# A hybrid layer pair in fp32 split form: triangular solve and state-space products in smaller array tiles, MLP loop written out

## The reference, cut to what matters

```
m = where(strict, einsum(kb, k) * decay, 0);  a_mat = m + eye(64)
sol = triangular_solve(a_mat, rhs, lower=True, unit_diagonal=True)
```

```
bu = einsum('bsgh,gph->bsgp', uf, b_bar)
states = associative_scan(combine, (lam_bar, bu))
y = einsum('bsgp,ghp->bsgh', states, c_mat).real + d * uf
```

## Time and profile before

| | |
|---|---|
| median of 3 runs | 2452.07 us (2451.09 to 2452.88) |
| profiled execution | 2454.28 us, of it the span of instructions 2452.5 us |
| PE busy | 2429.2 us |
| PEld busy | 1996.0 us |
| DVE busy | 1534.6 us |
| ACT busy | 1030.0 us |
| POOL busy | 274.8 us |
| granted TensorE clock, mean | 0.997 |

### The profile page before, as it was taken

One profiled execution on the slowest core, in us unless ns is written; L12 is line 12 of the kernel. 1 busy time (PEld: TensorE's weight loads), 2 busy tenths in 40 slices (PEclk: granted clock), 3 DMA queues, 4 the chain that ended last, 5 costly groups with the idle time before them and its releaser, 6 DMA issues.

```text
span 2452.5 us, 31953 instructions
## 1 busy us (share of the span) xinstructions
PE 2429.2 (99%) x13482; PEld 1996.0 (81%) x13482; DVE 1534.6 (63%) x1530; ACT 1030.0 (42%) x860; POOL 274.8 (11%) x226
## 2 busy tenths in 40 slices
PE   8999999999999999999999999999999999999998
PEld 7888888878888888888888888887777778888886
DVE  6465556557676455445445567789999955446564
ACT  4553345334344443443443434443433444544332
POOL 1002201210000000000000000054556400000000
PEclk9999999999999999999999999999999999999999
DMA  6343354346755455555555555665555576566753
GB/s 257 135 164 115 136 184 168 108 149 245 262 193 184 177 189 190 188 189 191 186 191 194 187 196 205 224 242 192 189 187 194 187 284 234 173 240 227 257 197 137
DMA packets 84220, 475.10 MB, mean 194 GB/s; under 512 B 8704, under 2 KB 8832, under 8 KB 32512
## 3 DMA queue, kind: packets, MB, share of 16 engines
q1 hardware_dynamic: 84096, 473.32, 54.2%
HBM read 450.21 MB, written 23.07 MB: 193 GB/s over the span
## 4 chain that ended last, share of the span: by engine, by line
PE 96%; DMA 1%; DVE 1%; ACT 1%; issue 0%; SPq 0%; DVEq 0%; ACTq 0%
PE acc L2098 29%; PE acc L2100 29%; PE acc L2099 29%; PE banks L2262 3%; PE banks L2111 2%; PE banks L2318 1%; DMA raw<-in_w 1%; PE banks L2385 1%; PE banks L2398 1%; DVE w_lo L1272 0%; ACT w_hi L820 0%; DMA av<-spilled 0%; DVE stats L1324 0%; PE banks L2438 0%; PE banks L2420 0%; PE banks L2236 0%
## 5 line engine op out<-in xcount | busy, mean ns | idle before, releaser
L1272 DVE TENSOR_TENSOR w_lo<-raw,w_hi 128x2048 fp32r<-128x2048 f32 x394 | 908.1, 2308 | 552.7 <-ACT w_hi L820 551.5
L820 ACT ACTIVATE w_hi<-raw 128x2048 fp32r<-128x2048 f32 x394 | 751.8, 1914 | 591.0 <-DMA raw<-in_w 588.8
L2098 PE MATMUL acc<-w_hi,a_hi 128*128 128x512 f32 x2112 | 840.5, 398 | 5.8 <-DVE a_lo L1308 3.1
L2099 PE MATMUL acc<-w_lo,a_hi 128*128 128x512 f32 x2112 | 824.7, 390 | 0.0
L2100 PE MATMUL acc<-w_hi,a_lo 128*128 128x512 f32 x2112 | 824.4, 390 | 0.0
L2098 PEld LDWEIGHTS acc<-w_hi,a_hi 128*128 128x128 f32 x2112 | 397.3, 188 | 104.2 <-issue 15.3
L2100 PEld LDWEIGHTS acc<-w_hi,a_lo 128*128 128x128 f32 x2112 | 397.4, 188 | 84.9
L2099 PEld LDWEIGHTS acc<-w_lo,a_hi 128*128 128x128 f32 x2112 | 397.8, 188 | 78.5
L2098 PE MATMUL acc<-w_hi,b_hi 128*128 128x512 f32 x928 | 364.2, 392 | 0.0
L2100 PE MATMUL acc<-w_hi,b_lo 128*128 128x512 f32 x928 | 361.5, 390 | 0.0
L2099 PE MATMUL acc<-w_lo,b_hi 128*128 128x512 f32 x928 | 361.2, 389 | 0.0
(11 more groups left out here) (356 smaller groups left out, 1642.4 us busy)
## 6 DMA issues: line engine op xcount, KB each, us to landing
raw<-in_w SPq DMA_DIRECT2D x395, 1024.0 KB, 4.8
spilled<-stage SPq DMA_DIRECT2D x72, 256.0 KB, 6.0
gate_in<-spilled SPq DMA_DIRECT2D x20, 512.0 KB, 5.8
x_rows<-in_x SPq DMA_DIRECT2D x4, 512.0 KB, 8.2
x_rows<-in_x SPq DMA_DIRECT2D x1, 2048.0 KB, 9.2
mem_rows<-in_mem SPq DMA_DIRECT2D x2, 1024.0 KB, 5.8
spilled<-stage_b SPq DMA_DIRECT2D x8, 256.0 KB, 5.9
out<-y_rows SPq DMA_DIRECT2D x3, 512.0 KB, 2.7
```

The costliest lines, as they stand in the source:

```text
L820: act.activation(w_hi[:, n % HIGH, :], raw[:, n % RAW, :], ACT.Copy)\
L1272: dve.tensor_tensor(w_lo[:, n % RAW, :], raw[:, n % RAW, :], w_hi[:, n % HIGH, :].bitcast(F32), ALU.subtract).then_inc(lo_split, 1)
L2098: pe.matmul(o, hi[:, tk], wh, start=first, stop=False)
L2099: pe.matmul(o, hi[:, tk], wl, start=False, stop=False)
```

## The change

1. **Solve.** The 64x64 matrix is worked as four blocks of 32x32. The diagonal blocks of M are packed, 32 columns to a matrix, so that levels 1 to 4 work on the two diagonal blocks alone. `by_block` issues them: eight matrices times four strips, 32 matmuls of 32x32 in four array tiles on the diagonal, 64 records. The last level uses the block off the diagonal (`across`, 16 matmuls of 32x32 a token tile). Both orientations of X lie side by side in one buffer, so DVE's subtractions and masks are one operation of 512 columns where they were two, and ACT's copy of Y and POOL's mask have 256 columns where they had 512. `solT` is zeroed by POOL, its diagonal blocks are written by POOL in four operations a token tile and its off-diagonal blocks by DVE in four. `turn` also turns the off-diagonal blocks and takes one more bank. The attention matrix is still transposed by `by_chunk`.
2. **State-space products.** PE makes `bu` for two steps in one go, eight matmuls in four row tiles out to four banks, at the even steps only; ACT copies the two banks of the odd step to `bu_odd`, and DVE reads them there. The outputs of two steps are made together as well, eight matmuls in four column tiles, at the even steps only. `s_out` gets a third buffer.
3. **MLP.** The loop is gone. Every unit is written out, its waits are against constants, the waits on bank and buffer readers that the loop left out are there again, and the hidden steps come from `schedule()` at the same distances.

The core of the diff:

```diff
-                if last_use[i] and me.it is None:
+                if last_use[i]:
...
-        def drive(me, slot_work, after_loop):
...
-                    with me.eng.Fori(0, LOOPS) as it:
...
+        def drive(slot_work):
+            for n in range(UNITS):
                 slot_work(n)
```

```diff
# PE
+            def by_block(b, at, lhs, rhs):
+                for k in range(8):
+                    for g in range(4):
+                        ins = pe.matmul(b[strip(g), at + 32 * k:at + 32 * k + 32], lhs(k, strip(g)), rhs(k, strip(g)),
+                                        start=True, stop=True)
+                return ins
+            def across(b, at, lhs, rhs, to):
+                for hd in range(4):
+                    for c in range(2):
+                        for d in range(2):
+                            first, second = strip(2 * c + d), strip(2 * c + 1 - d)
+                            src, dst = (first, second) if to == "second" else (second, first)
+                            ins = pe.matmul(b[dst, at + 32 * hd:at + 32 * hd + 32], lhs(d, hd, src), rhs(d, hd, src),
+                                            start=True, stop=True)
+                return ins
             def turn(half):
-                for z, x, to in (("M", MAT, "MT"), ("Q", ATT, "QT")):
-                    for t in range(NT):
-                        pe.wait_ge(dve_done, me.at(f"decay{half}{t}.{z}"))
-                        b = take_bank(f"turn{z}{half}{t}", 0, f"turn{half}{t}.{to}")
-                        by_chunk(b, per_chunk(t)[x], lambda k, rs: ident[rs, rs], f"turn{half}{t}.{z}")
+                for t in range(NT):
...
+                    by_block(b, 0, lambda k, rs: diagonal(m, k, rs), lambda k, rs: ident[rs, rs])
+                    by_block(b, 256, lambda k, rs: ident[rs, rs], lambda k, rs: diagonal(m, k, rs))\
+                        .then_inc(pe_done, me.done(f"turn{half}{t}.M"))
+                b = take_bank(f"turnC{half}", 0, f"turn{half}.Cc")
+                for t in range(NT):
+                    ins = across(b, t * P, lambda d, hd, rs: m[rs, 256 * d + 64 * hd + 32 * d:256 * d + 64 * hd + 32 * d + 32],
+                                 lambda d, hd, rs: ident[rs, rs], "first")
+                ins.then_inc(pe_done, me.done(f"turn{half}.C"))
+                for t in range(NT):
...
+                    by_chunk(b, per_chunk(t)[ATT], lambda k, rs: ident[rs, rs], f"turn{half}{t}.Q")
             def solve_y(half, n):
-                    by_chunk(b, w[SUM], lambda k, rs: w[INV][rs, 64 * k:64 * k + 64], f"solve{half}{t}{n}.Y")
+                    if n < LAST:
+                        ins = by_block(b, 0, lambda k, rs: block_of(w[SUM], k, rs), lambda k, rs: x_n(w, k, rs))
+                    else:
+                        ins = across(b, 0, lambda d, hd, rs: block_of(w[MAT], hd, rs), lambda d, hd, rs: x_n(w, 4 * d + hd, rs),
+                                     "second")
             def solve_x(half, n):
-                    by_chunk(b, w[MAT], lambda k, rs: w[EXP][rs, 64 * k:64 * k + 64],
-                             f"solve{half}{t}{n}.Z" if last else f"solve{half}{t}{n}.ZT")
-                    if not last:
-                        by_chunk(b, w[EXP], lambda k, rs: w[MAT][rs, 64 * k:64 * k + 64], f"solve{half}{t}{n}.Z")
+                    if n < LAST:
+                        by_block(b, 0, y, lambda k, rs: x_t(w, k, rs))
+                        ins = by_block(b, 256, lambda k, rs: x_t(w, k, rs), y)
+                    else:
+                        ins = across(b, 0, lambda d, hd, rs: y(8 + hd, rs), lambda d, hd, rs: x_t(w, 4 * d + hd, rs), "first")
             def ssm(i, part):
+                if i % 2:
+                    return
-                    b = [this_bank(g, f"bu{i}", g, f"ssm{i}.turned") for g in range(2)]
+                    b = [this_bank(q, f"bu{i}", q, f"ssm{i}.turned" if q < 2 else f"ssm{i + 1}.taken") for q in range(4)]
                     for z in range(2):
-                        for g in range(2):
-                            rs = slice(64 * (i % 2) + 32 * g, 64 * (i % 2) + 32 * g + 32)
+                        for q in range(4):
+                            ins = pe.matmul(b[q][:, z * T:(z + 1) * T], b_in[32 * q:32 * q + 32, ct, z, :],
+                                            uT[32 * q:32 * q + 32, ct, :], start=True, stop=True)
...
+                    b = this_bank(2, f"ssy{ct - 1}", 0, f"ssm{i}.ysum")
                     for z in range(2):
+                        for q in range(4):
+                            j = i - 2 + q // 2
+                            ins = pe.matmul(b[32 * q:32 * q + 32, 0:T], c_out[:, z, 2 * j + q % 2, :],
+                                            s_buf(j)[:, z, q % 2, :], start=z == 0, stop=z == 1)
# ACT
             def turn(half):
...
+                for t in range(NT):
+                    act.wait_ge(pe_done, me.at(f"turn{half}.C"))
+                    act.activation(per_chunk(t)[MAT][:, 0:P], bank_of(f"turnC{half}", 0)[:, t * P:(t + 1) * P], ACT.Copy)\
+                        .then_inc(act_done, me.done(f"turn{half}.Cc"))
             def ssm(i, part):
+                if i < 16 and i % 2 == 0 and part == 0:
+                    act.wait_ge(pe_done, me.at(f"ssm{i}.bu"))
+                    act.wait_ge(dve_done, me.at(f"ssm{i - 1}.turned" if i else "ssm0.turned"))
+                    for g in range(2):
+                        act.activation(bu_odd[:, g], bank(2 + g), ACT.Copy).then_inc(act_done, me.done(f"ssm{i + 1}.taken"))
# POOL
             def solve_x(half, n):
+                if n == 1:
+                    pool.memset(solT[:, :, :, :], 0.0).then_inc(pool_done, me.done(f"solT{half}.zero"))
# DVE
             def ssm(i, part):
+                    bu = [(bu_odd if k else banks[:, 0:2])[:, :, z * T:(z + 1) * T] for z in range(2)]
+                    if k:
+                        dve.wait_ge(act_done, me.at(f"ssm{i}.taken"))
+                    else:
+                        dve.wait_ge(pe_done, me.at(f"ssm{i}.bu"))
```

More of the change, by code:

```diff
@@ L132, in mask_constants @@
     out["upto"] = np.concatenate([packed(r <= c), packed(r >= c), packed(r <= c)], 1)
[L133 to L135 removed]
+    quarter = lambda m: np.concatenate([m[0:32, 0:32]] * 4, 0)
+    first = lower[0]
+    out["unit"] = quarter(r == c)
+    out["level"] = np.concatenate([quarter(x) for x in (first.T, first, first, first.T)] +
+                                  [quarter(x) for m in lower[1:5] for x in (m.T, m)], 1)
     out = {k: v.astype(np.float32) for k, v in out.items()}
@@ L232, in schedule @@
     put(end(f"w_mlp_down{p}", 2) - 2, "load_g_final")
-    put(end("w_mlp_up", 2 * p), "hidden", p, 0)
-    put(end("w_mlp_up", 2 * p + 1), "hidden", p, 1)
+    for p in range(1, NPIECE):
+        put(end("w_mlp_up", 2 * p), "hidden", p, 0)
+        put(end("w_mlp_up", 2 * p + 1), "hidden", p, 1)
     put(end("xa_wv", 1) + 2, "ssm_small", 0)
@@ L312, in at @@
         assert len({key for key, _ in marks}) == 1, names
-        return self._in_loop(marks[0][0], max(value for _, value in marks))
+        return max(value for _, value in marks)
     def here(self):
         assert self.count > 0
-        return self._in_loop(self.key, self.count)
+        return self.count
 KB = 1024
@@ L797, in _ @@
                     run_steps(me, steps, 2 * n + 1)
-                n += 1
-                if n != LOOP0 and n not in ends:
-                    run_steps(me, steps, 2 * n)
-                    run_steps(me, steps, 2 * n + 1)
+                if n + 1 not in ends:
+                    run_steps(me, steps, 2 * n + 2)
+                    run_steps(me, steps, 2 * n + 3)
             for t, n0, n1 in FINAL_DVE:
@@ L1833, in ssm @@
                 c_, s_ = rot[:, k, 0], rot[:, k, 1]
-                so = [s_out[:, k, z] for z in range(2)]
+                so = [s_buf(i)[:, z] for z in range(2)]
                 if i <= 15 and part == 0:
@@ L2374, in ssm @@
             def ssm(i, part):
-                if i <= 15 and part == 0:
-                    ct = i // 2
+                if i % 2:
+                    return
+                ct = i // 2
+                if i < 16 and part == 0:
                     pe.wait_ge(loaded["b_in"], 16)
```

224 lines of the change are left out of this document (88 added, 136 removed).

## The result

| | before | after |
|---|---|---|
| median | 2452.48 us (4 runs) | 2493.39 us (4 runs, 2491.97 to 2494.64) |
| profiled execution | 2454.28 us | 2494.64 us |
| mean granted clock | 0.997 | 0.984 |

The ratio is 1.0166, 95% interval 1.0152 to 1.018. The forecast was 2409 us with a range to 2455: wrong in sign.

What follows compares the result with a forecast made beforehand. The prediction took PE's instruction list, laid end to end, as the bound. From the profiled 2454.28 us it took 19.3 (state-space) and 24.1 (solve), giving 2410.9, or 2409 us against the median of the runs; range 2402 to 2455.

Steps and rivals of the forecast that it cites:

- The rate of small records: Solve: a 32x32 record holds its tile 31.7 ns, so with four tiles overlapping it costs 7.9 ns.
- The solve's sum: Solve: bursts fall from 67.4 us to 43.3 us over both halves, a gain of 24.1 us.
- 7.9 ns if nothing else holds it: Solve: cost taken for each small record in four tiles, between bounds of 7 and 29.2 ns.
- the supply rival: Solve: PE's issue of instructions limits all tiles together to 29.2 ns a record; 60 us more there, about 2493 us; chance 0.15.
- doubles at 128 and 256 columns, so it is the tile that sets it there: Argument against an instruction supply limit: the 29.2 ns a record comes from the array tile.
- The clock: New solve bursts: no falls to half clock counted; two in `turn` would cost 3.4 us.
- It fell to half once: Kernel before: one clock fall, after 2.7 us of decay sums, for 3.41 us, costing 1.7 us.
- The state-space part: State-space products: four tiles overlap, so merged bursts take 19.9 us instead of 39.2, a gain of 19.3 us.
- DVE is busy for 40.39 of them ... Cost 0: State-space steps: DVE needs 41.0 us a pair against PE's 40.7, a deficit of 0.3 us that never reaches PE.
- The bound given for DVE: State-space steps: with a DVE deficit of 2 us a pair, PE would lose some 5 us; kept for the range.
- The loop: MLP: writing out the loop costs 0, with bounds of -0.5 and +1 us.
- The rule of 25 ns between starts: Contrary rule: matmuls start no closer than about 25 ns; across all tiles, 3968 records cost 99 us, giving 2476 us.

Runs made afterwards that it cites:

- the probe: Kernel before with the MLP loop written out, plus twelve bursts of small matmuls waiting for nobody between MLP units; 1024 records in four 32x32 tiles: 28.5 ns a record.
- no_rot: Kernel before with written-out MLP and merged state-space products, but without GpSimd's rotation tables from step 2 on (those of steps 0 and 1 reused); 2433.93 us.
- loop_solve: Changed kernel with the state-space products as they were before, so only the new solve and the written-out MLP; 2488.79 us, ratio 1.0147.

## Why the prediction was wrong

**The rate of small records: right.** 7.9 ns forecast, 8.9 measured in `turn`, 8.6 in the probe (1.10 us for 128), as long as PE has the instructions; a record in one tile of 32x32 at 31.7 ns against 31.8. Four tiles overlap, in the solve and in both state-space products (1.27 us against 1.28).

**The solve's sum: wrong.** "43.3 in all, a gain of 24.1 us" holds for what the records take when they run. Three things on top, over both halves: 36.3 us of waits (33.4 in L2256, 1.1 for "issue" and 1.8 for VectorE in L2230) and 54 us at half the clock, in stretches of 3.4 to 10.2 us behind the stalls, worth up to 27. -24.1 + 36.3 + 27 = +39, against +36.6 in the markers; the part of the slow stretches that fell into stalls cost nothing.

**The failing step** is the one that made "7.9 ns if nothing else holds it" a cost, and put the supply rival at 0.15 with the argument that a record "doubles at 128 and 256 columns, so it is the tile that sets it there". The tile does set it at 29.2; but records that each take 29.2 ns could not show a supply that was hardly faster (28.5), and no burst of the kernel before has shorter ones in any number. The runs put in its place 36.3 us of waits and up to 27 us of clock. That rival gave 2493 us, the measured time, with nearly the right rate. Part of that is luck: it had the solve at +60 and the state-space part at -19.3, where they are +36.6 and +6.8, and it slowed every burst, where those of up to some 200 records often run at full rate.

**The clock: wrong.** "I count none; two in `turn` would be 3.4 us." A burst of 128 small records in four tiles leaves the clock up (1.00 from 891 to 898 us in the probe); where PE stalls after more of them, it falls. "It fell to half once" is a misreading of the kernel before as well: a second stretch at half the clock lies at 2008.03 us, again 3.41 us long. No term of the sum rests on it.

**The state-space part: wrong.** PE's own gain of 19.3 us is real (`no_rot`). The step "DVE is busy for 40.39 of them ... Cost 0" took a busy time that depends on the neighbour for a property of VectorE. The bound given for DVE, 5 us lost of the gain, was far too small: DVE was busy for 44.15 us of each pair of 44.25, and the gain of 19.3 became a loss of 6.8.

**The loop: right,** 0 us, though 13 more blocks of instructions are fetched (107 against 94).

**The rule of 25 ns between starts**, which the prediction took from the Trainium skill's "TensorE: Matmul & The Clock Gate", doesn't hold across tiles: in four tiles records start 8 to 9 ns apart. It would have warned rightly for a wrong reason.

## What to carry to other kernels

Count instructions, not only engine time: here 256 of PE's, that is 128 matmul records with their loads, arrive each 3.65 us or so. A run of records that each take under 28 ns goes on only as long as what is in hand, 169 to 242 records after a long quiet stretch and as few as 8 behind another burst (`loop_solve`, at 489.6 us); then it stalls, and stalls of several us cost clock too. The larger matmuls, at half the number of records, were faster than both orders of the small ones tried here.

A busy time read beside another engine is not that engine's own. Before a copy is moved from PSUM to SBUF under VectorE, look at what GpSimd does in that stretch; before an engine is called "just fast enough", look at how much of its time is its neighbour's, best by a run without the neighbour.

## What the runs showed of the hardware

In the probe PE had between 169 and 242 records (338 to 484 instructions) in hand at the start of a burst, and received 128 at a time, 3.5 to 4.0 us apart. A one-tile burst of 32x32 without any stall brought the clock down as well, while two tiles of 64x64 and four tiles with 128 moving columns left it up. Windows of the probe: two tiles of 64x64, four tiles with 128 moving columns, one tile.

```profile
1314.70:1331.00 16.30, 15.85 (x514) 15.37 (x513) 5.87 (x4) 3.29 (x2) 0.00 (x0) 1.00 0.21 68
1347.50:1354.60 7.10, 7.10 (x258) 6.90 (x257) 2.30 (x2) 3.31 (x2) 0.00 (x0) 1.00 0.42 150
1449.70:1461.70 12.00, 12.00 (x258) 11.94 (x257) 4.58 (x2) 3.23 (x2) 0.00 (x0) 0.61 0.23 90
```
